# GpSimd takes over one low-part subtraction for two tiles of a decoder layer's handover into the FFN

## The reference

```
    mix = jnp.concatenate([ret_out, conv_out], axis=-1) @ w_out
    h = h + rms_norm(mix, n_mix_post)
    xf = rms_norm(h, n_ffn_pre)
    gate, up = jnp.split(xf @ w_ffn_in, [D_FF], axis=-1)
    h = h + rms_norm((jax.nn.silu(gate) * up) @ w_ffn_out, n_ffn_post)
```

## Time and profile before

| | us |
|---|---|
| median of three runs | 1178.29 (1177.98 to 1179.56) |
| the profiled execution | 1177.31 |
| its span, first to last instruction | 1175.4 |

### The profile page before, as it was taken

One profiled execution on the slowest core, in us unless ns is written; L12 is line 12 of the kernel. 1 busy time (PEld: TensorE's weight loads), 2 busy tenths in 40 slices (PEclk: granted clock), 3 DMA queues, 4 the chain that ended last, 5 costly groups with the idle time before them and its releaser, 6 DMA issues.

```text
span 1175.4 us, 22876 instructions
## 1 busy us (share of the span) xinstructions
PE 1148.9 (98%) x8646; PEld 1129.1 (96%) x8646; DVE 802.2 (68%) x1242; ACT 444.3 (38%) x798; POOL 610.2 (52%) x455
## 2 busy tenths in 40 slices
PE   8999999999999999799999999999999999999997
PEld 7999999999999986699999999999999999999997
DVE  6368999954555247987685858584848585867646
ACT  6454454232334336642424233333333233333313
POOL 2066788304122357566565656474747473737316
PEclk9999999999989999899999999999999999999999
DMA  9311111111154223212121211212121212121134
GB/s 292 118 36 55 37 54 55 37 48 55 41 149 117 90 90 127 73 37 73 37 72 36 65 42 44 64 36 71 36 71 36 71 36 71 36 71 36 55 143 165
DMA packets 102360, 84.53 MB, mean 72 GB/s; under 512 B 2722, under 2 KB 89378, under 8 KB 102298
## 3 DMA queue, kind: packets, MB, share of 16 engines
q1 hardware_dynamic: 102258, 83.68, 23.2%
q10 hardware_dynamic: 48, 0.10, 0.0%
HBM read 72.86 MB, written 11.38 MB: 72 GB/s over the span
## 4 chain that ended last, share of the span: by engine, by line
PE 85%; DVE 5%; POOL 5%; issue 3%; DMA 2%; ACT 1%; DVEq 0%; SPq 0%; POOLq 0%; ACTq 0%
PE ps L409 26%; PE ps L411 26%; PE ps L410 26%; DVE w_ring L1601 1%; DMA f_raw<-in_w_ffn_in 1%; POOL o_last L825 1%; POOL h_ring L783 1%; PE ps L1965 1%; PE ps L1895 1%; PE ps L1914 1%; POOL st L616 1%; PE ps L2019 1%; PE ps L2018 1%; DMA x_st<-in_x_prompt 1%; DVE x_lo L1595 0%
## 5 line engine op out<-in xcount | busy, mean ns | idle before, releaser
L1737 DVE TENSOR_TENSOR ffn_acc<-ps,ffn_acc 128x516 f32<-128x516 f32 x264 | 183.6, 696 | 8.0 <-PE ps L411 2.6
L409 PE MATMUL ps<-xn_hi,w_hi 128*128 128x350 f32 (+2 forms) x576 | 187.2, 325 | 0.9 <-DVE xn_lo L1296 0.9
L411 PE MATMUL ps<-xn_lo,w_hi 128*128 128x350 f32 (+2 forms) x576 | 185.2, 322 | 0.0
L410 PE MATMUL ps<-xn_hi,w_lo 128*128 128x350 f32 (+2 forms) x576 | 184.9, 321 | 0.0
L409 PE MATMUL ps<-x_hi,w_ring 128*128 128x256 f32 x616 | 175.5, 285 | 5.8 <-DVE e_s L1615 3.8
L409 PE MATMUL ps<-x,w_ring 128*128 128x260 f32 x616 | 175.4, 285 | 1.6 <-issue 1.2
L410 PE MATMUL ps<-x,w_ring 128*128 128x260 f32 x616 | 175.3, 285 | 0.0
L411 PE MATMUL ps<-x,w_ring 128*128 128x260 f32 x616 | 175.0, 284 | 0.0
L410 PE MATMUL ps<-x_hi,w_ring 128*128 128x256 f32 x616 | 174.1, 283 | 0.0
L411 PE MATMUL ps<-x_lo,w_ring 128*128 128x256 f32 x616 | 174.1, 283 | 0.0
L409 PE MATMUL ps<-act_hi,w_ring 128*128 128x258 f32 x560 | 158.2, 283 | 0.1
(11 more groups left out here) (257 smaller groups left out, 2672.4 us busy)
## 6 DMA issues: line engine op xcount, KB each, us to landing
f_raw<-in_w_ffn_in SPq DMA_DIRECT2D x42, 512.0 KB, 3.9
raw<-in_w_in SPq DMA_DIRECT2D x24, 512.0 KB, 3.9
f_raw<-in_w_ffn_out SPq DMA_DIRECT2D x22, 512.0 KB, 4.1
x_st<-in_x_prompt SPq DMA_DIRECT2D x8, 512.0 KB, 8.6
raw<-in_w_out SPq DMA_DIRECT2D x8, 512.0 KB, 6.6
h_ring<-in_x_prompt SPq DMA_DIRECT2D x8, 512.0 KB, 4.1
h_scratch<-h_ring SPq DMA_DIRECT2D x8, 512.0 KB, 3.1
h_fin<-h_scratch SPq DMA_DIRECT2D x8, 512.0 KB
```

The source lines that it names most:

```text
L409: nc.tensor.matmul(out, hi, mhi, start=first, stop=False, skip_group_check=resumes)
L410: nc.tensor.matmul(out, lo, mhi, start=False, stop=False, skip_group_check=resumes)
L411: return nc.tensor.matmul(out, hi, mlo, start=False, stop=last, skip_group_check=resumes)
L1737: v.tensor_tensor(a, tile_banks(i), a, ALU.add).then_inc(s_acc, 1)
```

## The change

Of the two subtractions of `x_sums_lo`, the one for rows 20 to 27 (the second pair of sums) moves from VectorE to GpSimd for tiles 5 and 7. For tiles 1, 3 and 8 VectorE keeps both. GpSimd issues it at the end of its step 8 (tile 5) and of its step 10 (tile 7), behind its other work of these steps. TensorE's waits are adapted: the low parts of VectorE are counted two less for the second half of the tokens, and the product k = 4 waits in addition for GpSimd's two, which count on the semaphore `s_clo`.

In the diff the first two pieces are GpSimd's, the third VectorE's and the last TensorE's:

```
+SPLIT_SUMS = (5, 7)

+            def x_sums_lo(t):
+                xh, xl, xs = x_block(t)
+                pool.wait_ge(s_xs14, t // 2 * 2 + 2)
+                pool.wait_ge(s_shi, t // 2 * 2 + 2)
+                g.tensor_tensor(xl[:, 20:28], xs[:, 20:28], xh[:, 20:28].bitcast(F32), ALU.subtract).then_inc(s_clo, 1)
...
                 if t >= 2 and (t % 2 or t == 10):
                     x_sums_14(t - 2)
+                if t in (8, 10):
+                    x_sums_lo({8: 5, 10: 7}[t])
...
-                for i, q in enumerate((12, 20)):
+                for i, q in enumerate((12,) if t in SPLIT_SUMS else (12, 20)):
...
-                            pe.wait_ge(s_slo, 2 * pairs - 1)
+                            pe.wait_ge(s_slo, 2 * pairs - 1 - len(SPLIT_SUMS) * ss)
                         elif p == 4:
-                            pe.wait_ge(s_slo, 2 * pairs)
+                            pe.wait_ge(s_slo, 2 * pairs - len(SPLIT_SUMS) * ss)
+                            if ss:
+                                pe.wait_ge(s_clo, len(MIX_TILES) + 1 + len(SPLIT_SUMS))
```

## The result

| | before | changed |
|---|---|---|
| median | 1178.81 us | 1181.52 us |
| the profiled execution (span) | 1177.31 us (1175.4) | 1181.65 us (1179.8) |

The ratio of changed to before is 1.0024, 95% interval 1.0016 to 1.0031: 2.8 us slower (1.9 to 3.7), where 2.0 us had been forecast. In a second comparison (e10) it was 1.0021 (1.0012 to 1.0030). Each median is that of 14 executions, of which one was far longer than the rest (1874.06 us before, 1603.78 us changed) and is left out of the ratio. The median of 1181.52 is 1.2 us above the forecast of 1180.3, and half a microsecond of that is the kernel before, whose median over 14 executions is 1178.81 in place of the 1178.29 of the first three. It lies inside the range of 1177.4 to 1182.9, and just outside the 0.2% within which I had put the larger part of the chance.

A forecast was written before the change was run, and what follows sets the result against it. VectorE's list was taken to set the pace up to 504.69 us, TensorE's work behind it. + 1.06 - 1.14 + 2.1 = + 2.0 us on the 1178.29 us median gave 1180.3 us, range 1177.4 to 1182.9.

The forecast's parts named there:

- VectorE sets the pace up to k = 6, and nothing gives it back: Handover's last steps: VectorE's list paces up to 504.69 us; behind that TensorE has no waits to swallow a loss.
- Tile 5: a loss of 1.06 us in place of a gain of 1.14: Step 8: GpSimd's subtraction holds the lock 2.24 us, so VectorE loses 1.06 us where it was to save 1.14.
- of two engines with work in hand each gets one instruction: VectorE and GpSimd sharing SBUF: the lock is held for a whole instruction and changes hands in turn.
- the order of issue decides: Shared SBUF port pair of VectorE and GpSimd: issue order, not shape, decides who blocks; a 0.68 us instruction took 1.77.
- L1611 at some 2.9 us: Sign of being right: VectorE's instruction behind tile 5's subtraction takes some 2.9 us in place of 0.68.
- Tile 7: - 1.14 + 2.1: Step 10: VectorE saves 1.14 us, then loses 2.1 as the ninth tile's small subtractions wait for GpSimd's second subtraction.
- The sum of 2.0 us: At 504.69 us both tiles' terms, + 1.06 - 1.14 + 2.1, make the kernel 2.0 us slower.
- TensorE's clock as a rival: The new 2.5 us gap before 498.95 us lowers TensorE's clock again: 2.2 us more, 1182.5 us; chance 0.13.
- a granted clock of 0.50 between 498 and 507 us: Sign of being wrong: TensorE's clock at the 1.2 GHz level anywhere between 498 and 507 us.
- Offloading works: Both places: GpSimd's subtraction doesn't stop VectorE, which saves 2.28 us; 1176.0 us; chance 0.11.
- One site is free: At 496.6 or 480.6 us GpSimd lands beside a PSUM-reading instruction, one wait goes: some 1178.2 us; chance 0.12.
- The wait at k = 4: TensorE's new wait ends nothing: GpSimd's second subtraction is done at 498.75 us, k = 4 starts past 503.

The follow-up runs named there:

- e10: The changed kernel profiled and timed again, nothing altered; ratio to the kernel before 1.0021 (1.0012 to 1.0030).
- e1: Changed kernel with only tile 5's second low part on GpSimd, tile 7's staying on VectorE; ratio to before 1.0008 (0.9998 to 1.0019).
- e2: Changed kernel with only tile 7's second low part on GpSimd, tile 5's staying on VectorE; ratio to before 1.0006 (0.9992 to 1.0020).
- e9: As e7, plus tile 7's subtraction on GpSimd in step 10 ahead of the ninth tile's second sums; ratio to before 1.0012 (1.0001 to 1.0022).
- e4: Changed kernel with GpSimd writing zeros by memset in place of subtracting, in both places; ratio to before 0.9976 (0.9967 to 0.9986).
- e7: Changed kernel with only tile 5's subtraction on GpSimd, moved to step 9 beside VectorE's PSUM instructions; ratio to before 0.9990 (0.9981 to 0.9999).
- e5: Changed kernel with 16 transposes into an unused PSUM bank ahead of TensorE's product k = 1; ratio to before 1.0006 (0.9997 to 1.0015).
- e12: e1 with a power over 128 rows x 1 column between GpSimd's 8-row residual add and tile 5's subtraction; one run, 1180.22 us.
- e8: Changed kernel with tile 3's second low part on GpSimd instead of 5's and 7's, behind a 128-row add; ratio to before 1.0000 (0.9990 to 1.0010).
- e11: e7 once more, nothing altered; ratio to the kernel before 0.9988 (0.9978 to 0.9998).

## Why the prediction was right, step by step

- **VectorE sets the pace up to k = 6, and nothing gives it back.** Right: 669.17 and 669.21 us from k = 7 to the end.
- **Tile 5: a loss of 1.06 us in place of a gain of 1.14.** The size was right (1.17 in e1). The order was not: I had VectorE getting its turn between L783 and L701 and its next instruction standing. In fact its L1605 stood through both (4.57 us) and L1611 had its 0.68 us. The step "of two engines with work in hand each gets one instruction" failed here, and so did the sentence that the order of issue decides: L1605 had started at 480.50, L701 only at 481.63, and L701 went first. The sign named for this place, L1611 at some 2.9 us, did not come (0.68 us, behind L701 and not beside it). The sum hardly hangs on it, as one of the two waits out GpSimd's subtraction in either order.
- **Tile 7: - 1.14 + 2.1.** Right: + 0.85 alone (e2) and 0.86 on top of e1. The place too: the ninth tile's two tiny subtractions took 2.45 us, where some 2.3 had been written for the first. L701 took 2.80 us there in place of 2.2, since it first waited for VectorE's low parts of weights (L1611, until 497.80).
- **The sum of 2.0 us.** Right on VectorE: 2.03 and 2.04 in two profiles. The kernel lost 2.8 and 2.5 us. The start that was to move from 504.69 to 506.7 came at 509.12, or 508.0 without the 1.10 us ahead of L1550; of the 1.3 too much 1.2 are the clock's. What is above the 2.0 I ascribe in part to the next point; the intervals reach down to 1.4, so the times alone don't show that there is a rest.
- **TensorE's clock as a rival, at a chance of 0.13 and a price of 2.2 us.** Mis-sized both ways. The prediction named a granted clock of 0.50 between 498 and 507 us as a sign of being wrong, and the changed kernel's first profile has it. It fell there and in e2 and e9, not in e10, so it is rather a coin toss than one in eight; and it costs 1.2 us and not 2.2, since it was low for about 3.3 us (501.3 to 504.6) in place of the 5.4 that I had carried over from k = -4 and -3. Half of 1.2 brings 2.0 to 2.6. With this weighed in, the chance of more than 0.2% should have been above one half.
- **The other rivals.** "Offloading works" fell by e1 and e2 and is true where GpSimd doesn't read (e4), and for the larger part where VectorE's instructions beside it have an operand in PSUM (e7). "One site is free" fell, both cost about the same.
- **The wait at k = 4.** Free, as said: the second L701 ended at 500.01, ahead even of k = 1 (500.22), and in e4 the same wait stands in a kernel that is faster than before.

## What to carry to other kernels

Before work is moved from VectorE to GpSimd, look at what VectorE does in the moment in which GpSimd will do it: if those instructions have two operands in SBUF, VectorE pays GpSimd's time of the piece (here 2.3 us) in place of its own (1.1 us), and the more idle engine makes the kernel slower. Look for a stretch of VectorE with an operand in PSUM, as long as GpSimd's piece, tie the start to it by a semaphore, and look also at where GpSimd's next instructions then fall, since they can stop VectorE in turn. And a gap of some 2 us that is opened on TensorE may cost its clock on top.

## What the runs showed that I had not expected

**Who gets the turn.** Behind an add over 8 rows, GpSimd's next instructions went ahead of a VectorE instruction that had waited for 1.1 us: one in the changed kernel, e1, e5 and e10 (L1605 of 4.56 to 4.58 us), two in a row in e12 (5.07 us). Behind an add over 128 rows VectorE got its turn (2.28 us in e8, and in the earlier trace rows). It also did behind the 8 rows where a memset followed (e4), but the memset didn't stop it at all, so e4 says nothing on turns. Whether the 8 rows do it is open: no run here has an add over 128 rows in that very place, or one over 8 rows in another.

**Where the scatter of this kernel comes from.** Between 336 and 356 us, in a part that no kernel here alters, TensorE is busy throughout and its clock falls to 0.50 for a time that differs from run to run: it is 0.50 from 344 to 350 us before, from 342 to 350 in the changed kernel and from 342 to 354 in e1, with a little more at both ends. Before, changed, e1 and e11:

```profile
336.00:356.00 20.00, 20.00 (x147) 20.00 (x146) 10.75 (x21) 9.47 (x15) 4.76 (x3) 0.83 0.78 210
```

```profile
336.00:356.00 20.00, 20.00 (x136) 20.00 (x135) 9.13 (x17) 8.96 (x14) 4.75 (x3) 0.74 0.72 202
```

```profile
336.00:356.00 20.00, 20.00 (x125) 20.00 (x124) 8.44 (x18) 7.65 (x12) 4.76 (x3) 0.66 0.76 211
```

```profile
336.00:356.00 20.00, 20.00 (x144) 20.00 (x143) 11.32 (x23) 8.58 (x12) 5.62 (x4) 0.83 0.73 197
```

The scaling of the ninth tile starts at 475.88 and 475.00 us where the mean is 0.83, at 476.98 with 0.74 and at 479.88 with 0.66. The other eight profiles fit in: 477.02 to 477.70 with 0.74 (e2, e5, e7, e9, e12), 478.41 to 480.37 with 0.66 (e4, e8, e10). The 1.10 us between before and changed are already there at 378 us, and they still are 1.10 at the scaling:

```profile
377.81 0.60 PE L1949 MATMUL ps<-t_sm,ys 128*8 128x128 f32 x4 [1.60 <-ACT u L1015]
```

```profile
378.91 0.60 PE L1959 MATMUL ps<-t_sm,ys 128*8 128x128 f32 x4 [1.60 <-ACT u L1025]
```

Over the changed kernel's runs the mean clock of the whole span goes along with the time: 1179.26 and 1179.49 us at 0.992, 1182.50 and 1184.51 at 0.988. In e10's runs it hardly does (1182.22 us at 0.992), so the clock need not be the only source. Some four us of scatter hide a change of one or two; the distance between two instructions of VectorE in one trace, the stretch of the table above, repeated to 0.02 us for the two kernels that were profiled twice (23.11 and 23.12, 20.27 and 20.29).
